# A two-block float32 transformer on one core: an input projection that takes its rows before they are normalised, and an earlier load of x

## The reference, cut to what matters

```
h = x * rsqrt(mean(x * x) + eps) * attn_norm[l]
c_q, c_kv, k_r, q_d, k_d, v_d = split(h @ w_in[l])
```

## Time and profile before

| | |
|---|---|
| median of 3 runs | 1762.23 us (1757.72 to 1763.09) |
| the profiled execution | 1756.48 us, its span 1754.7 us |
| TensorE clock over the span | 0.977 of full |
| TensorE matmul / weight load | 1633.3 us (93%) / 1483.3 us (85%) |
| VectorE | 1065.0 us (61%) |
| ScalarE | 889.4 us (51%) |
| GpSimd | 193.1 us (11%) |
| DMA | 301 MB, 172 GB/s on average |

### The profile page before, as it was taken

One profiled execution on the slowest core, in us unless ns is written; L12 is line 12 of the kernel. 1 busy time (PEld: TensorE's weight loads), 2 busy tenths in 40 slices (PEclk: granted clock), 3 DMA queues, 4 the chain that ended last, 5 costly groups with the idle time before them and its releaser, 6 DMA issues. The chain is left out here.

```text
span 1754.7 us, 30271 instructions
## 1 busy us (share of the span) xinstructions
PE 1633.3 (93%) x12864; PEld 1483.3 (85%) x12864; DVE 1065.0 (61%) x1472; ACT 889.4 (51%) x1193; POOL 193.1 (11%) x138
## 2 busy tenths in 40 slices
PE   3998898999999999987899999988999999789999
PEld 0887567999999999956899999768999997679999
DVE  1698566554455445966644455766776557557773
ACT  2444555544454445555544445655655456556552
POOL 1140000122002210300122100000111000001110
PEclk8999999999999999999999999989999999899999
DMA  9244556566546554562376554223455542235553
GB/s 376 100 160 152 193 216 225 193 222 249 200 169 219 188 187 161 190 235 103 103 238 197 178 177 149 73 77 119 171 192 200 179 141 81 73 107 184 194 184 108
DMA packets 45110, 301.04 MB, mean 172 GB/s; under 512 B 5216, under 2 KB 7360, under 8 KB 11696
## 3 DMA queue, kind: packets, MB, share of 16 engines
q1 hardware_dynamic: 44304, 297.57, 47.9%
q0 software_dynamic: 240, 0.79, 0.1%
q10 hardware_dynamic: 432, 0.75, 0.1%
HBM read 298.02 MB, written 1.06 MB: 170 GB/s over the span
## 5 line engine op out<-in xcount | busy, mean ns | idle before, releaser
L1795 DVE TENSOR_TENSOR wl<-raw,wh 128x2064 fp32r<-128x2064 f32 (+3 forms) x236 | 531.6, 2255 | 478.3 <-ACT wh L1566 418.4
L1566 ACT ACTIVATE wh<-raw 128x2064 fp32r<-128x2064 f32 (+3 forms) x236 | 440.1, 1869 | 239.6 <-PE bank L1372 146.0
L1367 PE MATMUL bank<-hx_hi,wh 128*128 128x256 f32 x1920 | 544.5, 284 | 10.4 <-ACT hx_hi L1566 6.3
L1370 PE MATMUL bank<-hx_hi,wl 128*128 128x256 f32 x1920 | 537.3, 280 | 4.3 <-DVE wl L1795 3.9
L1372 PE MATMUL bank<-hx_lo,wh 128*128 128x256 f32 x1920 | 536.4, 279 | 0.0
L1367 PEld LDWEIGHTS bank<-hx_hi,wh 128*128 128x128 f32 x1920 | 364.7, 190 | 17.6 <-issue 17.2
L1370 PEld LDWEIGHTS bank<-hx_hi,wl 128*128 128x128 f32 x1920 | 364.8, 190 | 11.2 <-DVE wl L1795 6.7
L1372 PEld LDWEIGHTS bank<-hx_lo,wh 128*128 128x128 f32 x1920 | 364.8, 190 | 0.7 <-DVE hx_lo L1787 0.2
L1370 PE MATMUL bank<-hid_hi,wl 128*128 128x256 f32 x880 | 244.3, 278 | 3.1 <-DVE wl L1795 3.0
L1367 PE MATMUL bank<-hid_hi,wh 128*128 128x256 f32 x880 | 244.0, 277 | 0.9 <-ACT wh L1566 0.9
L1372 PE MATMUL bank<-hid_lo,wh 128*128 128x256 f32 x880 | 243.7, 277 | 0.0
(11 more groups left out here) (208 smaller groups left out, 1903.3 us busy)
## 6 DMA issues: line engine op xcount, KB each, us to landing
raw<-in_wts SPq DMA_DIRECT2D x208, 1032.0 KB, 4.9
raw<-in_wts SPq DMA_DIRECT2D x50, 1024.0 KB, 6.1
raw<-in_wts SPq DMA_DIRECT2D x20, 776.0 KB, 4.2
raw<-in_wts SPq DMA_DIRECT2D x4, 584.0 KB, 3.7
tmp<-tscr SPq DMA_DIRECT2D x16, 128.0 KB, 4.3
raw<-in_wts SPq DMA_DIRECT2D x2, 648.0 KB, 3.9
xTc<-in_ctxT SPq DMA_DIRECT2D x1, 1024.0 KB, 10.8
xTx<-in_xT SPq DMA_DIRECT2D x1, 1024.0 KB, 9.4
```

The costliest lines, as they stand in the source:

```text
L1367: pe.matmul(out, block(f, M.wh, k, ncols, c, m), x_hi, start=first and k == 0 and o == 0, stop=False, skip_group_check=True)
L1370: pe.matmul(out, block(f, M.wl, k, ncols, c, m), x_hi, start=False, stop=False, skip_group_check=True)
L1566: return act.activation(out, in_, func, bias=bias, scale=scale)
L1795: tt(M.wl[k][:, 0:ne], M.raw[f["r"]][:, 0:ne], M.wh[k][:, 0:ne].bitcast(F32), ALU.subtract).then_inc(*on.inc(f["tlo"]))
```

## The change

1. At the start, x is loaded ahead of piece 8 instead of piece 9. `p.look()` is gone; "nfin" of c is done in two parts (2 chunks, then 6) with the split of piece 8 alone between them (`p.one()`), and the split of piece 10 follows where `take` plans it, behind "nfin" of x. The sum of squares of x is not pooled on GpSimd: all four pairs go to matmuls, 8 in place of 5.
2. In the second block "nfin" is gone. `ffn_down` of the layer before writes, behind each pair's residual and squares, x times gain in two parts ("nraw": two ScalarE and two VectorE instructions of 128 x 256 for a pair). W0 starts from these. The root (`n.root`) comes behind W0's product, kept in a buffer of its own.
3. Every bank of W0 to W6 that needs it is multiplied in place by the root on VectorE ("scaled", 128 x 512; for W2 two instructions of 256 columns) before the ScalarE steps that read it. The v pieces (W7, W8) are scaled in the copy on ScalarE, in two instructions, by a transposed root (`rsT`: two transposes on TensorE and a small copy on VectorE, behind W1).

```diff
-    for n, dst, src, t in ((2, M.xT["c"][:, :, :], "ctxT", t_x["c"]), (9, M.xT["x"][:, :, :], "xT", t_x["x"]),
+    for n, dst, src, t in ((2, M.xT["c"][:, :, :], "ctxT", t_x["c"]), (8, M.xT["x"][:, :, :], "xT", t_x["x"]),
...
+    def one(self):
+        if self.pieces is not None:
+            self.prep(self.next + 1)
...
-    p.look()
     for pr in range(4):
         n["x"].add(pr, t_x["x"])
-    for s in "cx":
-        toks[s] = finish0(s)
+    begin0("c")
+    n["c"].apply(2)
+    p.one()
+    n["c"].apply(8)
+    begin0("x")
+    n["x"].apply(8)
...
             t = add_resid(s, b, tk, ch, gate, gate_tok, ready)
...
                 nrm.add(ch, t)
+                if unscaled:
+                    nrm.unscaled(ch, t, *unscaled)
...
-        toks = n.finish(M.V(("an", l)), None, a, hfree["x"], [t, t_vec])
+        toks, rsT, t_rsT = n.raw, None, ev("rsT")
...
+        def scaled(b, tk, parts=((P, 0, 512),)):
+            t = [ev("scaled") for _ in parts]
+            step("scaled", b=b, tk=tk, parts=parts, t_rs=n.t_rs, t=t)
...
                 b, tk = p.gemm_pair(("in2", l, 3 + j), a, toks)
                 run_pending()
+                t_s = scaled(b, tk)
...
-                rest = heads_norm(b, tk, M.V(("gdq" if j < 2 else "gdk", l)), 64, M.bones, None, None,
+                rest = heads_norm(b, t_s, M.V(("gdq" if j < 2 else "gdk", l)), 64, M.bones, None, None,
                                   dst[:, 2 * i:2 * i + 2, :], rf)
...
         ba, ta = p.gemm_pair(("in2", l, 0), a, toks)
+        n.root(rs)
+        ta = scaled(ba, ta)
         bb, tb = p.gemm_pair(("in2", l, 1), a, toks)
+        br, t_r = banks.get(), ev("mm")
+        step("rsT", b=br, free=br.free, t_rs=n.t_rs, rsT_free=list(rsT_free), t_r=t_r, t=t_rsT)
...
+        tb = scaled(bb, tb)
         f = take(("in2", l, 2))
         bc = banks.get()
         tc = p.gemm(f, 8, 160, [(0, P, 0, bc), (64, 96, T, bc)], a, toks)
+        tc = scaled(bc, tc, ((P, 0, T), (96, T, 2 * T)))
...
+    def scaled(b, tk, parts, t_rs, t):
+        on.wait_ge(tk, t_rs)
+        for (rows, lo, hi), done in zip(parts, t):
+            o = b.t[0:rows, lo:hi].rearrange("p (a t) -> p a t", t=T)
+            r = M.rs[0:rows, :].unsqueeze(1).to_broadcast([rows, (hi - lo) // T, T])
+            tt(o, o, r, ALU.mult).then_inc(*on.inc(done))
```

More of the change, by code:

```diff
@@ L408, in add, with unscaled, root @@
             self.n += 1
-            sums = [ev("nacc") for _ in range((1, 2, 0, 0)[self.n - 1])]
-            if self.n == 1:
+            sums = [ev("nacc") for _ in range((1, 2, 0, 0)[self.n - 1] if self.pooled else 0)]
+            if self.n == 1 and sums:
                 self.acc = q
             step("nsq", s=self.s, pair=pair, n=self.n, q=q, free=q.free, acc=self.acc, ready=list(ready), t=t,
-                 sums=sums, before=None if self.n == 1 else self.t_acc)
+                 sums=sums, before=self.t_acc)
             if sums:
                 self.t_acc = sums[-1]
-            if self.n == 2:
+            if sums and self.n == 2:
                 tmps.give(q, self.t_acc)
-            elif self.n > 2:
+            elif not sums:
                 self.late.append((q, t))
-        def root(self):
-            b, r = banks.get(), tmps.get()
+        def unscaled(self, pair, ready, gain, out, out_free):
+            toks = [(ev("h_hi"), ev("h_lo")) for _ in range(2)]
+            step("nraw", s=self.s, pair=pair, ready=ready, gain=gain, out=out, free=list(out_free), toks=toks)
+            self.raw += toks
+        def root(self, r=None):
+            b, r = banks.get(), r or tmps.get()
             t, t_ln, self.t_rs = ev("mm"), ev("ln"), ev("rs")
@@ L427, in root, with begin, apply @@
                 tmps.give(q, t)
-            tmps.give(self.acc, t)
+            if self.acc:
+                tmps.give(self.acc, t)
             banks.give(b, t_ln)
             self.rs = r
-        def finish(self, gain, shift, out, out_free, ready):
+        def begin(self, gain, shift, out, out_free, ready):
             if self.rs is None:
                 self.root()
-            us, toks, t_us = [], [], []
-            for c in range(9):
-                if c < 8:
+            self.toks = []
+            self.to = dict(gain=gain, shift=shift, out=out, free=list(out_free), ready=ready)
+        def apply(self, upto):
+            first = len(self.toks)
+            us, t_us = [], []
+            for c in range(first, upto + 1):
+                if c < upto:
                     u = tmps.get()
@@ L440, in finish @@
                     t_us.append(ev("nu"))
-                if c:
+                if c > first:
                     a, b = ev("h_hi"), ev("h_lo")
[L443 to L448, removed]
+                    tmps.give(us[c - 1 - first][0], a, b)
+                    self.toks.append((a, b))
+            step("nfin", s=self.s, rs=self.rs, t_rs=self.t_rs, first=first, us=us, t_us=t_us, toks=self.toks[first:],
+                 **self.to)
+            if upto == 8:
+                tmps.give(self.rs, t_us[-1])
+        def finish(self, *args):
+            self.begin(*args)
+            self.apply(8)
+            return self.toks
     t_vec, cst_tok = ev("ld_vec", 16), ev("ld_cst", 16)
@@ L1633, in poolproj, with nraw, vscaled @@
                scale=M.vcol(("pscale", l), j)).then_inc(*on.inc(t_x[j]))
+    def nraw(s, pair, ready, gain, out, free, toks):
+        on.wait_ge(ready, free)
+        for j in range(2):
+            c = 2 * pair + j
+            fn(out[0][:, c, :], M.xT[s][:, c, :], ACT.Copy, scale=gain[:, c:c + 1]).then_inc(*on.inc(toks[j][0]))
+    def vscaled(dst, b, tk, t_rsT, free, t):
+        on.wait_ge(tk, t_rsT, free)
+        for j in range(2):
+            fn(dst[:, j, :], b.t[:, j * T:j * T + T], ACT.Copy, scale=M.rsT[:, j:j + 1]).then_inc(*on.inc(t[j]))
     def vcopy(dst, b, tk, free, t, **_):
@@ L1796, in split, with nraw @@
            ALU.subtract).then_inc(*on.inc(f["tlo"]))
-    def nfin(s, rs, t_rs, us, t_us, toks, gain, shift, out, free, ready, **_):
-        on.wait_ge(t_rs, ready)
[L1800 to L1807, removed]
+    def nraw(s, pair, ready, gain, out, free, toks):
+        for j in range(2):
+            c = 2 * pair + j
+            on.wait_ge(ready, free, toks[j][0])
+            stt(out[1][:, c, :], M.xT[s][:, c, :], gain[:, c:c + 1], out[0][:, c, :].bitcast(F32), ALU.mult,
+                ALU.subtract).then_inc(*on.inc(toks[j][1]))
```

84 lines of the change are left out of this document (59 added, 25 removed).

## The result

| | before | changed |
|---|---|---|
| median | 1758.55 us (10 runs) | 1751.17 us (10 runs, 1749.67 to 1755.95) |
| ratio | 1 | 0.9955 [0.9943, 0.9967] |
| the profiled execution | 1756.48 us | 1751.69 us, its span 1749.9 us |
| TensorE clock over the span | 0.977 | 0.979 |

A ratio of 0.9955 is 7.9 us less (10.0 to 5.8): faster, by a little more than the 0.3% bound. A second measurement beside other runs gave 0.995 [0.9938, 0.9963].

The account below looks back on a forecast made before the run. TensorE, busy 93% of the span, was taken as the bound, so only its own order of work and waits count. Start -6.7 plus 2 x 1.1 for the layers gives -4.5 us: 1757.7 us on the median, range 1746 to 1765.

Parts of the forecast that it names:

- The start: Kernel start: product with x ends 8.8 us earlier, at 51.8; 2.1 given back waiting for piece 10's split; -6.7 us.
- Each later load hangs on TensorE's own progress and moves with it: Behind the start: pieces 9 and 10 land in time and later loads move with TensorE, so the -6.7 us holds.
- The boundary: Both layer boundaries of the second block: W0 directly behind ffn_down, then the root; 8.3 us against 12.6, -4.3 each layer.
- The waits: Projection: new TensorE waits at "hn2", 3.2 us (W5), 0.8 (W4), 1.4 (W6), less 1.5 taken up; 3.9 us.
- The fall of the clock behind the wait: Projection, behind the 3.2 us wait at "hn2" of W5: TensorE's clock falls, costing 1.5 us.
- The sum of the block: Second block: -4.3 at the boundary plus 5.4 for waits and clock, +1.1 us each layer, bounds -4.3 and +4.
- The total: Whole kernel: -6.7 + 2 x 1.1 = -4.5 us against the profiled execution, 1752.0; on the median 1757.7.
- A: Rival, second block: products on the banks hidden behind the next matmul group; -15.3 us, 1746.9; chance 0.20.
- B: Rival, second block: waits come, but the clock holds or they are 1 us shorter each; -9.7 us, 1752.5; chance 0.20.
- C: Rival, start: wait before piece 10 slows the clock, VectorE's long conv work behind is the bound; -1 us, 1761; chance 0.15.
- D: Rival, second block: one product in a bank costs 1.4 us, deciding from about 1.0; slower, up to 1769.9; chance 0.10.

Follow-up runs that it names:

- e3_unscaled_heads: The changed kernel, but banks of W0, W1, W3 to W6 and W2's c_kv columns left unscaled; 0.9922 of the kernel before, -13.7 us.
- e1_start: The kernel before with only point 1 of the change (the start), second block as before; 0.9967 of the kernel before, -5.8 us.
- e6_fill: The changed kernel plus six matmuls that nobody reads on TensorE ahead of "hn2" of W5; 0.9968 of the kernel before.
- e2_block: The kernel before with only points 2 and 3 of the change (second block), start as before; 1.0004 of the kernel before, +0.7 us.
- e11_change_again: The changed kernel measured a second time, nothing altered, on the same chip as e12_w4_w6_again; 0.995 of the kernel before.
- e5_w4_w6: The changed kernel, but the banks of W4 and W6 left unscaled, W3 and W5 scaled; 0.9977 of the kernel before.
- e12_w4_w6_again: The kernel of e5_w4_w6 measured again beside the changed kernel on one chip; 0.9979 of the kernel before.

## Why the prediction was right, and where not

1. **The start: right at its end, at 52.06 where I had 51.8, with the wait for piece 10's low part.** I had -8.8 at the product and 2.1 given back; the profiles show -8.6 and 2.1 (106.7 less 104.6). By itself it measured -5.8 where I had -6.7. One figure on the way was off without an effect: the sixteen records of the root took 4.66 us where I had 6.0, beside the split.
2. **"Each later load hangs on TensorE's own progress and moves with it": this step failed.** The weights behind the loads at 190 us came 4.7 us earlier where TensorE had been ahead by 6.46, and 1.0 earlier where it had been ahead by 4.07.
3. **The boundary: right.** -4.3 for each layer forecast; 12.6 - 7.5 = -5.1 in layer 0. W0 took 5.53 (I had 5.6) and the root 1.97 (I had 2.4). The transposes stand behind W1 and are not in the 5.1; they begin at 1052.68 and the next product at 1052.82, so that about 5.0 is the number to set beside mine. `e3_unscaled_heads` against `e1_start` is -7.9 us for two layers, where I had -8.6.
4. **The waits: right at W5 and W6, not at W4.** 3.2 at "hn2" of W5, measured 3.03; 1.4 at W6, 1.53; about 1.5 taken up behind them, 1.56 (0.25 and none left of 0.54 and 1.27). At W4 I had 0.8 from a split that holds VectorE up. It held nothing up: VectorE had been idle for 1.44 us when W4's bank was done (row at 1089.97), and the 0.36 is what product and square in series take beyond TensorE's step in between. The fall of the clock behind the wait came too, in both layers, worth 1.45 us by `e6_fill` (forecast 1.5). In layer 1 the waits are 3.04, 0.36 and 1.56.
5. **The sum of the block**: from the end of ffn_down (before 1042.21, changed 1039.48) to the matmul of 1110.69 (changed: 1108.69) the lead shrinks from 2.73 to 2.00 us, so this part of the layer loses 0.7, where I had 1.1. `e2_block` measured +0.7 [-1.2, +2.8] for both layers, where I had +2.2.
6. **The total** was -4.5 against the profiled execution, and profile against profile it is 1751.69 - 1756.48 = -4.8. By medians it is -7.9, and its interval (5.8 to 10.0 less) does not reach -4.5. The difference is in how far one execution stands for many: that of before lay 2.1 us below the median of its ten runs, that of after 0.5 above. Nor does the absolute forecast, 1757.7 against 1751.17, fail by its steps alone: the median of three that it starts from is 3.7 us above that of the ten.
7. **That profile against profile gives my -4.5 is in part luck.** The terms of my sum don't stand in the profiles one behind the other. Lead over the profile of before in us, at the last residual instruction of `ffn_down` ahead of each layer of the second block (before: 1042.63 and 1395.83) and at the end of the span:

| | ahead of layer 0 | ahead of layer 1 | end |
|---|---|---|---|
| forecast | 6.7 | 5.6 | 4.5 |
| changed kernel | 2.7 | 0.0 | 4.8 |
| the same kernel, `e11_change_again` | 2.7 | 5.0 | 5.1 |
| `e1_start` | 0.0 | -1.8 | -0.7 |

The one program takes 355.9 us for layer 0 in one profile and 350.9 in the other. The stretch from 1140 to 1170 us, behind the wait of 4.4 us in the heads, has a mean granted clock of 0.77 in the first and 0.94 in the second, which is 5 us of full-speed time. What supports the terms is the medians of many executions (-5.8 for the start, +0.7 for the block) and the local readings above; the way from the start's 5.8 us to the small leads in single profiles was not followed beyond 200 us, and the profile of before is itself faster than all ten of its runs.

Of the rivals, A (the products hidden) is refuted by the wait of 3.03 us; what it promised, -15.3, is nearly what `e3_unscaled_heads` has, -13.7, with most products gone. The rule of the Trainium skill that stood beside it, "TensorE: Matmul & The Clock Gate", section "Loop structure matters more than you think" (VectorE's reading of PSUM does not break the warmth of TensorE, as the next group follows at once), does not describe this trace. The page has the next group follow at once, and here it could not: two engines stand between the bank and the next matmul, one with a split of 2.31 us in its queue, and behind the wait TensorE had a mean granted clock of 0.70 over 5.6 us. B lies nearest in time (-9.7), but its conditions, shorter waits or a held clock, were not met. C's condition was half met: the clock falls behind the wait on piece 10's split in six of the eleven profiles listed under "Where such gains go", among them one of the two of the changed kernel, and it then costs 1.5 us. Its other half named VectorE's work behind the start as the bound; what the second marker shows there is a load. D is refuted by 696 ns for a product; it needed 1.0 us.

## What to carry to other kernels

When a factor is moved out of a product, ask of each reader whether it cancels there: the banks that feed a norm need no scaling, and leaving it out at two places (W3, W5) turned the change from -7.9 to -12.5 us (3.7 to 4.6 us more, with an interval of some 3.4 either way). A cheap instruction (0.7 us) between a bank and its reader costs what stands ahead of it in the queue, and moving that (here the split of the next weight) only helps if it is not itself due next. A gain early in a kernel is kept only as far as the loads behind it come earlier too, so look for the next stretch at which a DMA ends the wait. And a sum of terms that meets the time of one profile is not yet shown: take a second profile of the same program, and see whether the terms stand where they should.

## What the runs showed of the hardware that I had not expected

- A VectorE product that reads and writes the same bank took 696 ns for 128 x 512, 12 ns more than the one into SBUF: hardly a price for the write into the bank.
- TensorE's clock does not follow the waits one by one. A wait of 1.6 us at 55 us was followed by a fall in one profile of the changed kernel and not in the other, and so it was with the kernel of `e5_w4_w6` and `e12_w4_w6_again`. This kernel has slightly fewer waits, and yet over all executions its mean clock was 0.974 against 0.977 beside it (medians) and its time 0.3% longer. Keeping TensorE busy through one wait raised the clock there from 0.70 to 1.00 and did not make the kernel faster.
